# Sparse attention loop with longer distances between the steps of one score tile

## The reference, cut to what matters

```
o_cmp, p_cmp = nsa_compressed(q, kv[:, :, 0], kv[:, :, 1], ...)      # 31 compressed keys
o_slc = nsa_selected(q, kv[:, :, 2], kv[:, :, 3], top_i, top_ok)     # selected blocks of keys
o_win = nsa_window(q, kv[:, :, 4], kv[:, :, 5])                      # keys in a window of 512
y_nsa = gb[..., 0:1] * o_cmp + gb[..., 1:2] * o_slc + gb[..., 2:3] * o_win
```

## Time and profile before

| | |
|---|---|
| median of 3 runs | 3122.21 us |
| the profiled execution's own time | 3124.37 us |
| its span on the core | 3122.5 us |
| PE busy | 2900.4 us (93%) |
| DVE busy | 1494.5 us (48%) |
| ACT busy | 886.2 us (28%) |
| POOL busy | 340.9 us (11%) |
| mean granted clock of TensorE | 0.963 |
| the four groups | from about 375 us to about 773 us, 100 us each |

### The profile page before, as it was taken

One profiled execution on the slowest core, in us unless ns is written; L12 is line 12 of the kernel. 1 busy time (PEld: TensorE's weight loads), 2 busy tenths in 40 slices (PEclk: granted clock), 3 DMA queues, 4 the chain that ended last, 5 costly groups with the idle time before them and its releaser, 6 DMA issues.

```text
span 3122.5 us, 34634 instructions
## 1 busy us (share of the span) xinstructions
PE 2900.4 (93%) x13386; PEld 2375.3 (76%) x13386; DVE 1494.5 (48%) x2168; ACT 886.2 (28%) x1206; POOL 340.9 (11%) x70
## 2 busy tenths in 40 slices
PE   6998799999989999899996799999999889899997
PEld 6777688888767888778885588887888765578886
DVE  2334344444456553465434744434453379555532
ACT  4333443344233222222221322222221232422211
POOL 4222111112300000000001000000000056100000
PEclk9998899999999999999998899999999999999999
DMA  6222112222342223222222123232222221122232
GB/s 194 81 65 68 54 44 78 71 71 69 120 155 68 94 94 98 91 81 94 95 97 77 59 90 106 88 101 86 99 98 90 86 68 41 62 74 94 94 98 71
DMA packets 255085, 270.43 MB, mean 87 GB/s; under 512 B 5695, under 2 KB 243407, under 8 KB 254858
## 3 DMA queue, kind: packets, MB, share of 16 engines
q1 hardware_dynamic: 250688, 261.77, 26.1%
q10 hardware_dynamic: 4298, 7.36, 0.6%
HBM read 258.62 MB, written 10.49 MB: 86 GB/s over the span
## 4 chain that ended last, share of the span: by engine, by line
PE 69%; issue 16%; DVE 6%; POOL 5%; ACT 2%; DMA 1%; SPq 0%; POOLq 0%; DVEq 0%; ACTq 0%
PE bank L1114 20%; PE bank L1115 20%; PE bank L1116 20%; POOL w_lo L1074 3%; POOL w_lo L1068 3%; PE bank L1566 1%; PE bank L1129 1%; PE bank L1131 1%; PE bank L1130 1%; DVE rstd L1989 1%; ACT w_hi L662 1%; PE bank L1142 1%; PE bank L1144 0%; PE bank L1143 0%; DVE w_lo L1954 0%
## 5 line engine op out<-in xcount | busy, mean ns | idle before, releaser
L1114 PE MATMUL bank<-h_hi,w_hi 128*128 128x512 f32 x2064 | 818.8, 397 | 54.3 <-POOL w_lo L1074 25.9
L1115 PE MATMUL bank<-h_lo,w_hi 128*128 128x512 f32 x2064 | 812.9, 394 | 0.0
L1116 PE MATMUL bank<-h_hi,w_lo 128*128 128x512 f32 x2064 | 811.7, 393 | 0.0
L1954 DVE TENSOR_TENSOR w_lo<-w_raw,w_hi 128x2048 fp32r<-128x2048 f32 (+2 forms) x176 | 390.2, 2220 | 391.7 <-ACT w_hi L662 325.7
L1114 PEld LDWEIGHTS bank<-h_hi,w_hi 128*128 128x128 f32 x2064 | 393.2, 191 | 145.3 <-POOL w_lo L1074 30.1
L1116 PEld LDWEIGHTS bank<-h_hi,w_lo 128*128 128x128 f32 x2064 | 393.1, 190 | 83.0
L1115 PEld LDWEIGHTS bank<-h_lo,w_hi 128*128 128x128 f32 x2064 | 393.2, 190 | 82.2 <-issue 1.2
L1114 PE MATMUL bank<-hid_hi,w_hi 128*128 128x512 f32 x880 | 343.9, 391 | 0.0
L1116 PE MATMUL bank<-hid_hi,w_lo 128*128 128x512 f32 x880 | 342.8, 390 | 0.0
L1115 PE MATMUL bank<-hid_lo,w_hi 128*128 128x512 f32 x880 | 342.7, 389 | 0.0
L654 ACT ACTIVATE w_hi<-w_raw 128x2048 fp32r<-128x2048 f32 x124 | 236.8, 1910 | 357.7 <-PE bank L1116 350.3
(11 more groups left out here) (355 smaller groups left out, 3448.2 us busy)
## 6 DMA issues: line engine op xcount, KB each, us to landing
w_raw<-in_ffn_w_in_dram SPq DMA_DIRECT2D x88, 1024.0 KB, 5.1
w_raw<-in_w_in_dram SPq DMA_DIRECT2D x32, 1024.0 KB, 5.3
w_raw<-in_ffn_w_out_dram SPq DMA_DIRECT2D x32, 1024.0 KB, 5.2
w_raw<-in_w_ffn_in_dram SPq DMA_DIRECT2D x22, 1024.0 KB, 5.1
w_raw<-in_ffn_w_out_dram SPq DMA_DIRECT2D x16, 768.0 KB, 4.5
w_raw<-in_conv_w_pw_dram SPq DMA_DIRECT2D x12, 1024.0 KB, 5.6
w_raw<-in_w_ffn_down_dram SPq DMA_DIRECT2D x8, 1024.0 KB, 5.1
gate_scratch<-gate_stage ACTq DMA_DIRECT2D x24, 256.0 KB, 2.0
```

Source lines behind the costliest of these rows:

```text
L1114: nc.tensor.matmul(bank[b][:, 0:n], wh, xh, start=first, stop=False)
L1115: nc.tensor.matmul(bank[b][:, 0:n], wh, xl, start=False, stop=False)
L1116: ins = nc.tensor.matmul(bank[b][:, 0:n], wl, xh, start=False, stop=last)
L1954: v.tensor_tensor(w_lo[slot][:, 0:n], raw[s][:, 0:n], w_hi[slot][:, 0:n].bitcast(F32), ALU.subtract).then_inc(w_lo_ready, 1)
```

## The change

The distances become names at the top of the file and grow: `turn` and its copy come three steps behind the score (before: two), `weigh` five (before: three), and `out_step` runs from iteration 10 on (before: 8). PE's loop gets 37 iterations (before: 35). The calls beside the steps (`high_in_loop`, `gate_evac`, the compressed exponential, the 3 gate products of each iteration) stay in the iterations that they had.

```
+TURN_LAG, WEIGH_LAG, OUT_LAG = 3, 5, 10
...
 # ACT
-                for i in range(NS + 2):
+                for i in range(NS + TURN_LAG):
                     if i < NS:
                         exp_step(i)
...
-                    if i >= 2:
-                        turn_step(i - 2)
+                    if i >= TURN_LAG:
+                        turn_step(i - TURN_LAG)
                     if i == 2:
                         high_in_loop(g * 2 + (U_NSA // 2 + 1), 0, 0)
...
 # PE
-                for i in range(NS + 3):
+                for i in range(NS + WEIGH_LAG):
                     if i < NS:
                         scores(i)
-                    if 2 <= i < NS + 2:
-                        turn(i - 2)
-                    if i >= 3:
-                        weigh(i - 3)
+                    if TURN_LAG <= i < NS + TURN_LAG:
+                        turn(i - TURN_LAG)
+                    if i >= WEIGH_LAG:
+                        weigh(i - WEIGH_LAG)
                     gates(GATE_STEP)
...
 # DVE
-                for i in range(NS + 5):
+                for i in range(NS + WEIGH_LAG + 2):
...
-                    if 2 <= i < NS + 2:
-                        turn_step(i - 2)
-                    if i >= 8 and i % HPG == 0:
-                        out_step(i // HPG - 2)
+                    if TURN_LAG <= i < NS + TURN_LAG:
+                        turn_step(i - TURN_LAG)
+                    if i >= OUT_LAG and (i - OUT_LAG) % HPG == 0:
+                        out_step((i - OUT_LAG) // HPG)
```

## The result

| | before | after |
|---|---|---|
| median, 6 runs each | 3121.31 us | 3134.54 us (3131.19 to 3135.76) |
| ratio after / before | | 1.0038, 95% interval 1.0026 to 1.0049 |
| the profiled execution's span | 3122.5 us | 3134.0 us |
| mean granted clock | 0.963 | 0.961 |

The change makes the kernel slower by 0.38%, some 12 us (the two medians differ by 13.2). The forecast was slower by 8, 3130 us in a range of 3121 to 3137.

What follows compares the result with a forecast made beforehand. PE, busy 2900 of 3122 us, was taken to bound the kernel. Moved gate products +6.2, loop waits -1.5 and clock +3.4 us sum to +8.1, a median of 3130 us, range 3121 to 3137.

Steps and rivals of the forecast that it cites:

- The walk: Loop iterations 2 to 5 and 16 to 19, followed through ACT's and PE's lists: 0.35 us a group won.
- the single waits: PE's loop waits at 411.02, 430.42 and 434.14 in group 1: nothing left of them with the longer distances.
- The 0.15 us at iteration 32: Copy of step 30 falls behind ACT's high part; the `weigh` that wants it waits 0.1 to 0.2 us.
- The six gate products at full price: Moved from tail into the loop, where PE has no gap: 1.55 us a group, 6.2 us over all.
- The tail's 3.40 us: First gate product to transposes, set by DVE's 16 additions: stays 3.40 us with three gate products instead of nine.
- +1.55 less 0.35 a group: Loop: cost of six moved gate products a group, less what the longer distances give back; +4.7 us without the clock.
- two of four tails: Lower clock lasting into the 48 dense products behind the tail, 1.7 us each, taken twice: +3.4 us.
- Rival (a): Clock in and behind the tails stays as it was: +4.7 us, 3127; 31 in 100.
- The Trainium skill's two rules: Tails: frequent brief PE idling swings the clock (sum +8.1 us), or only longer gaps harm (sum +4.7).
- Rival (b): Loop: ACT's high parts covered, all waits vanish: -7 us, 3115; half of it about -1; together 11 in 100.
- (c): Loop: six gate products fill its waits and cost nothing: time as before or 1.5 us less, 3121; 7 in 100.
- (d): Loop: late `turn` delays the next copy and `turn`, longer waits: +2.7 us a group, 3138; 5 in 100.

Runs made afterwards that it cites:

- the kernel with both repairs: Changed kernel without gate products in the two added iterations (nine in the tail) and with ACT's high parts one iteration later: 3113.05 us, ratio 0.9973.

## Why the prediction was right, and where it was off

- **The loop's waits.** The walk said: the single waits vanish, `turn` of step 2 waits 1.4 us and `turn` of step 16 1.2 us; 9 us by brackets. The trace has 1.33 and 1.01 in group 1, 9.8 us in all. Right, place by place, and the instructions named are those. The run with the high parts later shows the cause.
- **The 0.15 us at iteration 32** is there too, as four waits of `weigh` of 0.2.
- **The six gate products at full price.** The tail's 3.40 us stayed in all four groups, and with +1.55 less 0.35 a group the loops should have grown by 4.7; they grew by 6.0, of which 0.5 is group 4 alone. Right, a little low. The products themselves cost what the forecast says (6.3 us by the run with nine in the tail, forecast 6.2); it is the distances that gave back 0.3 us instead of 1.5 (that run's loops against those before). The filled tail, which takes the clock away, gives +5.5 for this part against the forecast's +4.7.
- **The clock.** This is the term that was mis-sized: two of four tails at 1.7 us, 3.4 in all. Measured: all three spacings between groups grew, by 1.8, 3.0 and 2.8 us, 7.5 in sum, with 0.9 more ahead of the transposes of group 3; filling the tail gave 7.5 back. The fall was taken for something that a tail has or hasn't; but it came in each of them, and in groups 1 to 3 it lasted past the transposes well into the queries (0.60, 0.68, 0.50). That is 4.8 of the 7.5 us; the forecast had no term for the compressed scores 20 us later, where the other 2.7 lie. How far the emptied tail causes this second part is open: the compressed scores took 4.4 to 5.7 us in the kernel with both repairs too, with nine products in each tail. The term is about double the forecast, and it, not the loop, decides that the change is clear of noise. Rival (a), the clock as it was, would have been 8 us too low.
- **The Trainium skill's two rules** (TensorE: Matmul & The Clock Gate) gave +8 and +4.7. The trace agrees with the one on brief idling between groups of matmuls in what comes of it: the two levels alternate and no pause in the tails is longer than 2.2 us. It does not bear out the reason, as the clock had fallen before PE paused in groups 1 to 3, and fell in the kernel with twelve products ahead of the transposes with no pause at all. The long waits that the "HAM oscillation" section tells of were not needed here.
- Rival (b), high parts covered, took place only in the kernel where they were moved. Rivals (c) and (d) did not: the tail's waits were not hidden, and no second wait followed in the loop.
- **The sum** was about 5 us short: the terms of the four groups measure +14.4 us in the profiles and the medians differ by 13.2, where the forecast had +8.1. "Two of four tails" was a choice that no row gave; that the sum with it comes nearer than rival (a) owes to the mechanism being right, and not to the working of its size.

A gain of 7.5 to 10 us was there for the taking, in three versions with nine products in the tail and one with twelve, once the filling was back.

## What to carry to other kernels

When a software pipeline is made deeper, write down in each engine's list what the moved instructions now stand behind: a copy that goes one iteration later can pass a long instruction that stayed, and the distance won is lost again. And count the filling: independent work that is dealt out per iteration goes where the iterations are, and is missing where it hid a wait that no distance in the loop touches. Judge such a place by starts or by matmuls per stretch with the granted clock beside it, since a busy share of 100% shows neither.

## What the runs showed of the hardware that I had not expected

- 24 useless dense products of 512 columns, placed into an idle stretch of TensorE, made the program 7.5 us faster.
- With three gate products in the tail the 48 dense query products behind the transposes took 11.6 to 13.0 us, in all nine cases of three kernels (the changed one, the one with old distances and the one with later high parts). With nine or more products there they took 11.0 to 11.2 in every case.
- The whole spacing from the transposes to the next loop hardly varies in those nine cases: 24.0 to 24.1 us. In the five kernels with nine gate products in the tail it is 20.9 to 22.8 us in 14 of 15 cases, and 24.0 in one.
- The clock fell in stretches where TensorE was busy the whole time. In group 1 of the kernel with twelve products ahead of the transposes it was 1.00 in the first 2.3 us of the products with the compressed values (16 products with 31 rows and 64 columns each) and 0.50 in the rest of them:

```profile
455.78:458.10 2.32, 2.32 (x22) 2.32 (x21) 0.91 (x5) 0.00 (x0) 0.03 (x1) 1.00 0.60 160
458.10:460.73 2.63, 2.63 (x14) 2.51 (x13) 0.00 (x0) 0.00 (x0) 0.00 (x0) 0.50 1.03 350
```
